# Low parts of the weight slots subtracted in two GpSimd operations of 512 columns

## Time and profile before

| | us |
|---|---|
| median of 3 runs (lowest to highest) | 3597.08 (3595.73 to 3599.03) |
| the profiled execution | 3597.62 |
| its span | 3595.8 |
| TensorE busy | 3505.1 (97% of the span), 19862 matmuls |
| VectorE busy | 1723.3 (48%) |
| ScalarE busy | 1359.1 (38%) |
| GpSimd busy | 1263.5 (35%), 599 instructions |
| mean granted clock of TensorE | 0.995 |

### The profile page before, as it was taken

How to read it: one execution, slowest core, us unless ns; L and a number is a source line. 1 busy time by engine, 2 the same in 40 slices (tenths; PEclk the granted TensorE clock), 3 DMA queues, 4 the chain that set the end, 5 groups by cost and what they waited for, 6 DMA issues and landing times.

```text
span 3595.8 us, 52717 instructions
## 1 busy us (share of the span) xinstructions
PE 3505.1 (97%) x19862; PEld 2706.1 (75%) x19862; DVE 1723.3 (48%) x2632; ACT 1359.1 (38%) x2322; POOL 1263.5 (35%) x599
## 2 busy tenths in 40 slices
PE   9999999999999999999999999999999989999998
PEld 7877787888788777788887677788854477767886
DVE  2655667443345665854335642603147764535042
ACT  3245524332323553333325544423215154444232
POOL 4422234444444223444443143344400022424443
PEclk9999999999999999999999999999999999999999
DMA  4421122223233111223332232232222301213222
GB/s 139 128 77 54 53 78 92 94 99 103 89 106 118 53 59 65 82 94 99 100 100 94 98 102 71 82 100 93 100 105 71 105 5 51 92 59 100 99 94 82
DMA packets 101561, 313.25 MB, mean 87 GB/s; under 512 B 26625, under 2 KB 26753, under 8 KB 100737
## 3 DMA queue, kind: packets, MB, share of 16 engines
q1 hardware_dynamic: 82080, 298.90, 24.8%
q10 hardware_dynamic: 19296, 11.76, 1.3%
HBM read 302.23 MB, written 5.24 MB: 86 GB/s over the span
## 4 chain that ended last, share of the span: by engine, by line
issue 43%; PE 35%; POOL 17%; DVE 2%; DMA 1%; ACT 1%; DVEq 0%; POOLq 0%; SPq 0%; ACTq 0%
POOL ring_r L2878 17%; PE ps L506 9%; PE ps L507 9%; PE ps L508 9%; PE ps L1200 2%; PE ps L1121 1%; PE ps L876 1%; PE ps L1050 1%; DMA ring<-in_weights 1%; PE ps L1076 1%; PE ps L1280 1%; PE ps L1236 0%; PE ps L1332 0%; DVE Z L2768 0%; DMA X<-in_x 0%
## 5 line engine op out<-in xcount | busy, mean ns | idle before, releaser
L2878 POOL TENSOR_TENSOR ring_r<-ring,rounded_r 128x1024 fp32r<-128x1024 f32 x501 | 1230.2, 2458 | 1938.0 <-ACT rounded_r L1381 1937.7
L506 PE MATMUL ps<-source_hi,rounded_r 128*128 128x512 f32 x2560 | 1021.7, 399 | 26.5 <-POOL ring_r L2878 6.5
L1381 ACT ACTIVATE rounded_r<-ring 128x1024 fp32r<-128x1024 f32 x504 | 533.6, 1059 | 1308.8 <-PE ps L508 1188.2
L507 PE MATMUL ps<-source_hi,ring_r 128*128 128x512 f32 x2560 | 999.3, 390 | 0.0
L508 PE MATMUL ps<-X_lo,rounded_r 128*128 128x512 f32 x1536 | 601.0, 391 | 0.0
L506 PEld LDWEIGHTS ps<-source_hi,rounded_r 128*128 128x128 f32 x2560 | 482.1, 188 | 156.8 <-issue 20.4
L507 PEld LDWEIGHTS ps<-source_hi,ring_r 128*128 128x128 f32 x2560 | 482.5, 188 | 96.0 <-issue 2.4
L508 PEld LDWEIGHTS ps<-X_lo,rounded_r 128*128 128x128 f32 x1536 | 289.6, 189 | 62.1
L508 PE MATMUL ps<-N_lo,rounded_r 128*128 128x512 f32 x768 | 299.2, 390 | 0.0
L2417 DVE SCALAR_TENSOR_TENSOR T<-ps,PAR,T 128x511 f32<-128x511 f32 (+1 forms) x176 | 131.5, 749 | 227.2 <-ACT T L1618 212.3
L506 PE MATMUL ps<-H_hi,rounded_r 128*128 128x512 f32 x512 | 199.2, 389 | 0.0
(11 more groups left out here) (490 smaller groups left out, 5125.6 us busy)
## 6 DMA issues: line engine op xcount, KB each, us to landing
ring<-in_weights SPq DMA_DIRECT2D x560, 512.0 KB, 3.3
X<-in_x SPq DMA_DIRECT2D x4, 512.0 KB, 7.0
PAIR<-Z ACTq DMA_DIRECT2D x32, 64.0 KB
out_x<-X SPq DMA_DIRECT2D x4, 512.0 KB, 2.7
SWAP<-Z ACTq DMA_DIRECT2D x4, 256.0 KB, 5.5
MEM<-in_mem ACTq DMA_DIRECT2D x1, 1024.0 KB, 4.8
mem_keys<-Z ACTq DMA_DIRECT2D x1, 1024.0 KB, 3.8
diag_in<-Y ACTq DMA_DIRECT2D x8, 128.0 KB, 2.2
```

Source lines behind the costliest of these rows:

```text
L506: mm(o, lh, rh, start=start, stop=False)
L507: mm(o, ll, rh, start=False, stop=False)
L1381: av(RH[:, j, :], ring[:, j, :], ACT.Copy).then_inc(w_hi, 1)
L2878: nc.gpsimd.tensor_tensor(RL[:, j, :], ring[:, j, :], RH[:, j, :].bitcast(F32), ALU.subtract).then_inc(w_lo, 1)
```

## The change

The subtraction of a slot is written as two operations of 512 columns (`S` is 512). The first has no semaphore; the second adds 1 to `w_lo`. Waits, other engines and the loads stay as they are.

```diff
             def remainder(split, j):
 
                 pool.wait_ge(w_hi, split + 1)
-                nc.gpsimd.tensor_tensor(RL[:, j, :], ring[:, j, :], RH[:, j, :].bitcast(F32), ALU.subtract).then_inc(w_lo, 1)
+                for e in range(2):
+                    h = slice(e * S, e * S + S)
+                    ins = nc.gpsimd.tensor_tensor(RL[:, j, h], ring[:, j, h], RH[:, j, h].bitcast(F32), ALU.subtract)
+                ins.then_inc(w_lo, 1)
```

## The result

The changed kernel took 3601.45 us in the median of 17 runs (3597.22 to 3609.02), the kernel before 3597.85 in 17 runs beside it (3594.01 to 3602.23). The ratio is 1.0014, with an interval of 1.0008 to 1.0020: slower by 5.0 us (2.9 to 7.2), less than the 0.2% that was to count as slower. The two medians alone are 3.6 us apart; in what follows, differences in us come from the ratio unless the text says otherwise. The profiled execution took 3600.21 us; its span is 3598.4 against 3595.8.

What follows compares the result with a forecast made beforehand. TensorE sets the pace in long matmul runs. Terms +3.4 + 4.2 + 0.8 - 0.6 - 1.8 - 0.4 = +5.6 us, less 0.6 absorbed, gave +5: about 3602 us; forecast's own range 3598 to 3606, overall 3594 to 3610.

Steps and rivals of the forecast that it cites:

- The cover: In long matmul runs, the 95 us of added GpSimd time over 501 slots stays hidden behind the matmuls.
- The second start: Each split subtraction costs 0.19 us more; it counts at TensorE's 18 waits for a slot: +3.4 us.
- The entries: At nine slot waits, a blocked VectorE operation gets between the halves, delaying the second by 0.47 us each: +4.2 us.
- the ninth: Slot wait at 1121.22, VectorE blocked on L2287: an operation getting between the halves delays the slot by 0.47 us.
- The 0.8 for a second slot at L2442: At four L2442 waits, the subtraction following at once adds its own extra operation start: 4 x 0.19 = +0.8 us.
- VectorE's gain: VectorE blocked about 1.2 us instead of 2.4: -0.6 at X waits, -1.8 at the queries' products, -0.4 at program start.
- the -0.4: At program start, TensorE's 1.85 us wait for X_lo shortens: -0.4 us booked, between 0 and 1.85.
- PE's wait for `ring_r`: TensorE's total wait for GpSimd's subtracted slots was to rise from 12.3 to about 19 us.
- No entry: Rival, chance 0.15: GpSimd keeps the port between halves, so VectorE gains without cost; only +4 us remains, 3601.
- The port freed is what counts: Rival, chance 0.1: all TensorE waits for N_lo go and the start gains; -10.4 + 4.2 = -6.2 us, 3591.
- The start is dear: Rival, chance 0.2: 0.32 us per slot, delays also at about 17 more slots, no recovery: +10 us, 3607.
- The subtraction hides wholly: Rival, chance 0.1: the second half's start overlaps the first's end and seam gains balance delays: no change, 3597.

Runs made afterwards that it cites:

- 461 slots in halves: Part of a kernel halving 472 of 501 slots, all but those in TensorE's way, against the kernel before: 3592.63 us, ratio 0.9986.
- experiment 1: The kernel before and the changed kernel, both unedited, measured and traced again: 3597.52 us (ratio 1.0000) and 3600.42 us (1.0007).
- the kernel with 11 slots: Against the kernel before, only 11 subtractions halved, where VectorE is blocked in work TensorE needs soon: 3593.22 us (0.9990), again 3594.95 us (0.9991).
- the 29 slots alone: Against the kernel before, only the 29 subtractions in TensorE's way halved, the 472 others whole: 3606.58 us, ratio 1.0020.

## Why the prediction held

The forecast was 3602, from +5 us, and the change cost +5.0 and, again, +2.5. By its steps:

- **The cover.** Right, and tested: 461 slots in halves cost nothing that shows.
- **The second start.** Right. The undisturbed pair takes 2.54 and not 2.59, 0.14 more than a whole subtraction. The five waits for a slot that no VectorE operation enters (603, 977, 1137, 1546, 1921) grew by 0.14 in the mean in the first pair of traces and by 0.28 in the second, 0.21 together, where 0.19 was booked.
- **The entries.** Right in mechanism at eight of nine sites, in size at the seams, and a quarter too high at L2442: start and entry together were 0.66 by the forecast and came to 0.69, 0.80, 0.61 and 0.61 at the four seams and 0.55, 0.61, 0.45 and 0.36 at L2442. The entry alone is 0.44 for 0.47: that is how much longer the second half becomes, in the median of the 69 slots of the changed kernel in which a two-input operation of 512 columns (TENSOR_TENSOR) stands blocked when the first half ends. L2154 there took 1.78 (1.7 forecast). The two seams were forecast at 2.0 and 2.2 and are 2.02 and 2.10. Wrong at the ninth, 1121: no wait at all in the first trace of the changed kernel and 0.86 in the second. Over the traces it is 0.06 to 0.75 in the four with that slot whole (0.71 in the kernel before) and 0.00 to 1.05 in the six with it in halves, 0.42 and 0.66 in the mean. The scatter is larger than the step, so the traces neither show its 0.66 nor exclude it.
- **The 0.8 for a second slot at L2442.** Not there: from 2200 to 2240 the matched matmuls lose 0.62, which is the one wait at 2225 (0.22 to 0.83).
- **VectorE's gain.** The walk through the queries' product ended at 0.9 each by the argument that X runs into the last half. It is 1.0 to 1.1, and for that reason: the 2.00 went almost whole, X ended 0.68 sooner where 0.9 was booked, and TensorE's next wait for N_lo gave 0.9 back. The sum of waits for N_lo fell by 2.2 and 2.9, at the low end of the 2 to 4 forecast. At 572.03 the wait went. At the start of the program the -0.4 is neither shown nor excluded: the waits for X_lo (L2097) add up to 2.5 to 4.6 in four traces with the slot there whole, 3.6 in the mean, and to 2.3 to 3.7 in six with it in halves, 3.0 in the mean.
- **PE's wait for `ring_r`.** "About 19": 18.8 and 18.5.
- **The rivals.** "No entry" has fallen: VectorE's operations come through after one half, and the slot is late by their length. "The port freed is what counts" had a gain of 10.4, three times what the kernel with 11 slots shows (3.6 and 3.2). "The start is dear" is refuted in its main term: the pair is 0.14 longer where it had 0.32, and the 461 slots in neither list cost nothing that shows; that waits add up without recovery was not tested by itself. "The subtraction hides wholly" has fallen too: the pair is 0.14 longer in the open, and the 29 slots alone cost 7.2. (The share of the forecast above 3604.3 was generous: 1.7 of the 8 us from 3598 to 3606 lie there, a fifth and not a third if the range is filled evenly.) For the 29 the terms of the sum, 3.4 + 4.2 + 0.8 = +8.4, stand against +7.2 measured; for the 11, -2.8 against -3.6 and -3.2.

What the sum did not have is the clock: I put a stretch more or less into the range, and did not see that the waits I lengthened are those behind which it falls. At the four seams the two traces of the changed kernel have one and three such stretches, 1.6 us each, those of the kernel before none; over all runs the clock is lower by what some 2 us make (experiment 1). The waits, for which the sum had +5.6, came to less: those for slots, N_lo, X_lo (L2097) and X (L585) together grew by 4.5 and 2.0 us in the two pairs of traces. The 0.8 is missing, the entries at L2442 were smaller, and the ninth site shows nothing clear. So the waits are right in mechanism and too large in sum, and the clock fills the gap: that the total comes out at 3602 is in part luck. How the +5 divides exactly stays open, since taking the stretches away in the changed kernel moved the time by less than the measurement tells.

The Trainium skill, TensorE: Matmul & The Clock Gate, section HAM oscillation — how this bites in real kernels, describes waits between groups of matmuls after which TensorE starts again at the low clock. The traces agree in kind: behind the waits for the last slot at the four seams, 16 of the 24 in kernels whose slot is in pieces there (waits of 2.0 to 3.3 us) were followed by 0.50, and none of the 24 in kernels whose slot is whole there (1.3 to 1.9).

## What to carry to other kernels

An operation of GpSimd that is hidden nearly everywhere is still priced by the few places where TensorE waits for its signal: list those, and split an operation only where it blocks someone, not where someone waits for its end. Cutting a long GpSimd operation lets VectorE in between the pieces, which helps whoever waits for VectorE and costs whoever waits for GpSimd nearly as much as the operation that enters is long, up to once per cut (0.44 us for 512 columns, 2.05 for 2048). And a wait of TensorE that is lengthened from 1.5 to 2 us can cost more than its 0.5 us: read the granted clock behind it.

## What was not expected of the hardware

- GpSimd's subtraction, float32 from float32 to rounded float32, took 0.32 us for 64 columns, 0.74 for 256, 1.29 for 512, 2.26 for 960 and 2.40 for 1024 (medians; 1259 ns was the shortest at 512 in the changed kernel). The line through 512 and 1024 has 2.16 ns per column and 0.18 us of start, and goes through the other three within 10 ns.
- At each boundary between two GpSimd operations a VectorE operation that is blocked gets in, even where the first is of 64 columns and the second stands right behind it with no wait. This held at every seam that I read; GpSimd in turn gets in before VectorE's next two-input operation, as before the X of 3071.47 and of 3078.28 above (1.6 us for 0.69).
- Of 16 waits of 2.0 to 2.5 us at the four seams 8 were followed by half clock, at the same places now yes, now no from trace to trace; of 8 waits of 2.8 to 3.3 us all 8. So the traces show the price of a stretch, and not at which idle time it comes.
